# Even layer of a two-layer sequence trunk: zeros stored in a tap table, tap matrices read back shifted, and the attention bias spread before the stream

## The chip, the cores and the metric

The kernel runs on one core of one Trainium2 chip. The metric is the device time of one execution in microseconds (us). Engines are named as in the profile: PE (TensorE matmul), PEld (TensorE weight load), DVE (VectorE), ACT (ScalarE), POOL (GpSimd) and SP (SyncE, which here issues nearly all DMAs).

## The reference

Two residual layers over a sequence of 2048 tokens of width 1024, float32, and a final norm. The change is in layer 0, the even layer:

```python
h = rmsnorm(x, norm_w[0])
u, g_a, q, k, v, g_b = split_cols(h @ ev_w_in, [512, 512, 512, 128, 128, 512])
a_out = s5_mixer(u, ...) * silu(g_a)           # 32 groups of 16 channels, one 64-dim complex state each
b_out = swa_mixer(q, k, v, sinks, rel_bias) * silu(g_b)
x = x + concat([a_out, b_out]) @ ev_w_out
# s5_mixer: bu = B_bar u;  states = scan(lam_bar, bu);  y = Re(C states) + d * u;  gelu, half-GLU
# rel_bias[h, q, j] = table[bucket(j - 64 - q), h]   (64 queries against 128 keys)
```

Layer 1, the odd layer, is gated linear attention; the change does not touch it.

## The kernel before

**Loop of the even layer.** The input projection is cut into 72 products `n` (18 column groups of 128, times 4 blocks of 512 tokens). Each product is 24 matmuls 128x512 and is written as two half steps, `p = 2n` and `p = 2n + 1`. Every engine has its own hand-written loop over `p` from 12 to 147 (SP line 507, ACT 828, DVE 1110, PE 1284), and other work is hung on given values of `p`: so the order of work on an engine, and in SP's DMA queue, is fixed by these loops, and the engines meet at semaphores. PE does the half product first and then the small work of its `p`.

**Start.** 16 tiles of `x` (128 tokens each) are loaded into three buffers (`load_x`), squared on ACT (`square`, L680), scaled on DVE (`normed`, L885), turned by PE (`turn_x`, L1176), and split into a rounded part on ACT (`upper`, L686) and a rest on DVE (`lower`, L891). The products start when four tiles are through. SP's order at the start is `x` tiles 0 to 2 with two weight blocks, then zeros into the pads of `k_pad` and `v_pad` (L495) and one store of zeros over all 32 tap matrices (L496, 2048 KB), then `x` tile 3 (lines 486 to 499). ACT's second evacuation waits for these zeros, because they lie in its staging tile (L703).

**S5 tables, p = 16 to 50.** The S5 layer works on blocks of 8 steps. For each of 32 groups it needs a 128x384 table in DRAM (`scr["tab"]`): the input matrix (`bm`), the tap matrix (block Toeplitz: block column k is the row of 8 taps shifted by 16 k, zeros ahead of it) and the output matrix (`cp`). They are made for two groups at a time, 16 batches `q`, each batch two half steps: DVE makes powers (`powers_of_b` L989 to 991 at `p = 16 + 2q`, `powers_of_c` L1004 to 1006 at 17), PE turns (`turn_b` L1204, 17) and multiplies (`taps` L1212, 18), ACT copies (`copy_bm` L742, 17; `copy_ker` L748, 18), DVE adds the skip term (`skip` L1016, 19), SP stores (`store_cp` L379, 17; `store_bm` L374, 18; `store_toep`, 20). `store_toep` runs for odd `q` alone: 8 DMAs for the four groups of two batches, one for each shift:

```python
dst = scr["tab"][2 * q - 2:2 * q + 2].rearrange("g p c -> p g c")
for k in range(TS):
    sp.dma_start(dst[k * GRP:(k + 1) * GRP, :, P + k * GRP:2 * P], ker[:, :, 0:P - k * GRP]).then_inc(toep_st, 16)
```

The tap tile `ker` holds two batches. So `copy_ker` of an even `q` waits until the 8 stores of the two batches before it have landed (L747), and `taps(q)` on PE waits for `copy_ker(q - 1)`. POOL makes cosine and sine tables in the same stretch, until 161 us.

**Stream, p = 37 to 139.** For each group `i`, at three half steps each, SP loads the table row (L405), cosines and sines (L406, one 64-row table read twice) and inputs (L409); the request waits until PE has done the outputs of group `i - 2` (`y_done`). PE multiplies (`inputs` L1221 at `p = 40 + 3i`, `outputs` L1228 and L1229 three half steps later), ACT and DVE do scan and gelu (`take_v`, `scan`, `turn_back`, `gelu_out`), SP stores (`store_g`).

**Attention, p = 76 on.** Ahead of it, at `p = 53`, `set_attention` loads the bias table, a one-hot matrix and four pieces of the sinks; `distances` on PE (L1233, p = 55) and DVE (L1060, p = 56) forms the bias by distance (8 heads x 191), `spread_distances` (L431, p = 57) stores it 64 times over, 382 KB, and `load_bias` (L442, p = 61) reads it back shifted.

Of the kernel before, what the change touches and what calls it, by code (L numbers as in the profile page):

```python
# [17 lines left out]
P = 128  # L18
# [3 lines left out]
NT = SEQ // P  # L22
# [11 lines left out]
GPI = 4  # L34
GLU_C = BLK // TS
# [141 lines left out]
def even_layer(nc, prm, scr, ht_hi, ht_lo, cst, base, glu):  # L177
# [46 lines left out]
    with ExitStack() as ctx:  # L224
# [14 lines left out]
        zeros = stage[:, 3, 0:P]  # L239
# [54 lines left out]
        table, oneh, dvec = (at("at_table", B + 24, [BUCKETS, HEADS]), at("at_onehot", B + 24.75, [BUCKETS, NREL]),  # L294
                             at("at_by_distance", B + 25.5, [HEADS, NREL]))
# [12 lines left out]
        ps_d = bank[2][0:HEADS, 0:NREL]  # L308
# [9 lines left out]
         bx_ready, zero_in, bp_ready, b_turned, bm_ready, bst, cp_ready, k_done, ker_copied, ker_ready, cqst, toep_st,  # L318
# [3 lines left out]
            "k_done", "ker_copied", "ker_ready", "cqst", "toep_st", "cs_made"))  # L322
        cs_st = c.sems("s5_cs_st", 2)
# [5 lines left out]
        (set_in, dist_ready, dist_sb, dist_out, bias_in, achain, s_done, m_ready, e_done, r_ready, p_ready, p_turned,  # L329
         pt_ready, v_turned, v_ready, o_done, o_read) = (c.sem("at_" + n) for n in (  # L330
            "set_in", "dist_ready", "dist_sb", "dist_out", "bias_in", "chain", "s_done", "m_ready", "e_done",
# [7 lines left out]
        CS_ALL, TAB_ALL, TOEP_ALL = 16 * 8, 16 * NQ, 128 * (NQ // 2)  # L339

        with nc.Block() as block:
            @block.sync
            def _(sp):
# [32 lines left out]
                def store_cp(q):  # L376
                    dst = scr["tab"][2 * q:2 * q + 2].rearrange("g p c -> p g c")
                    sp.wait_ge(cp_ready, q + 1)
                    sp.dma_start(dst[:, :, 2 * P:3 * P], cp[:, :, 1:, :].rearrange("p g s i -> p g (s i)")).then_inc(cqst, 16)  # L379
# [14 lines left out]
                def load_stream(i):  # L394
# [9 lines left out]
                    sp.wait_ge(toep_st, 128 * (i // 4 + 1))  # L404
                    sp.dma_start(tab[:, j], scr["tab"][i]).then_inc(ld[j], 16)  # L405
# [9 lines left out]

                def set_attention():
                    sp.wait_ge(bst, TAB_ALL)
                    sp.wait_ge(cqst, TAB_ALL)
                    sp.wait_ge(toep_st, TOEP_ALL)
                    with nc.allow_non_contiguous_dma(reason="small parameters"):  # L420
                        sp.dma_start(table[:], prm["rel_bias_table"]).then_inc(set_in, 16)
# [1926 lines left out]
```

## Time and profile before

| | us |
|---|---|
| runs before, median of 3 (lowest to highest) | 1743.18 (1741.81 to 1743.65) |
| the profiled execution's own time | 1737.88 |
| its span, first to last instruction | 1736.1 |
| busy in the span: PE, DVE, ACT, POOL | 1651.5, 855.7, 630.5, 282.0 |
| mean granted TensorE clock | 0.990 |

PE is busy for 95% of the span. The even layer's loop lies between 38 and 612 us, the odd layer behind it. Each row of the trace gives start, duration, engine, line, operation and tile; a bracket at the end is the idle time of the engine ahead of it and what ended it.

### The profile page before, as it was taken

The page shows a single profiled execution, that of the slowest core. Times are in us where ns is not written, and L with a number is a line of the kernel's source. Part 1 is how long each engine was busy: PE and PEld are TensorE (multiplying, and loading weights), DVE is VectorE, ACT ScalarE, POOL GpSimd, SP SyncE. Part 2 cuts the span into 40 slices and gives each one's busy share as a digit, 9 for nine tenths or more (in the row PEclk, how much of TensorE's full clock was granted, in tenths as well). Part 3 has the DMA queues.
Part 4 walks back from the last instruction along what each step waited for, and adds up shares of the span by engine and source line. Part 5 has one row for each costly group of instructions (what it writes and reads, how often), then busy time and mean ns, then how long its engine had stood idle before and what let it go on. Part 6 is the DMA issues. An engine that isn't in the chain of part 4 may idle for free.

```text
span 1736.1 us, 22665 instructions
## 1 busy us (share of the span) xinstructions
PE 1651.5 (95%) x7910; PEld 1336.4 (77%) x7910; DVE 855.7 (49%) x1704; ACT 630.5 (36%) x1586; POOL 282.0 (16%) x500
## 2 busy tenths in 40 slices
PE   3998889999999979999999999999999999999997
PEld 2776667777777757888768888888888888878886
DVE  4868543476676556553363333333433444354443
ACT  4622233466666655332263122222222332132221
POOL 1866000000000071110000022221222211000000
PEclk9999989999999989999999999999999999999999
DMA  7335444454445595322233333333333332366663
GB/s 220 124 118 164 121 134 124 143 151 151 135 141 151 156 274 180 137 87 84 99 104 117 118 106 125 103 109 111 106 125 101 99 118 82 104 214 193 193 194 109
DMA packets 272009, 235.51 MB, mean 136 GB/s; under 512 B 81752, under 2 KB 225048, under 8 KB 271896
## 3 DMA queue, kind: packets, MB, share of 16 engines
q1 hardware_dynamic: 260600, 232.94, 42.8%
q10 hardware_dynamic: 11296, 1.12, 0.5%
q8 instruction: 64, 1.05, 0.3%
q14 instruction: 49, 0.40, 0.1%
HBM read 140.09 MB, written 93.91 MB: 135 GB/s over the span
## 4 chain that ended last, share of the span: by engine, by line
PE 61%; DVE 1%; ACT 1%; DMA 0%; issue 0%; POOLq 0%; POOL 0%; ACTq 0%; DVEq 0%
PE odd_bank L2140 29%; PE odd_bank L2186 10%; PE odd_bank L2295 10%; PE odd_bank L2165 2%; PE odd_bank L2245 2%; PE odd_bank L2242 1%; PE odd_bank L2243 1%; PE odd_bank L2224 1%; PE odd_bank L2149 1%; PE odd_bank L2200 1%; PE odd_bank L2226 0%; PE odd_bank L2253 0%; PE odd_bank L2227 0%; PE odd_bank L2252 0%; PE odd_bank L2228 0%; DMA scr_heads<-odd_ga_min 0%
## 5 line engine op out<-in xcount | busy, mean ns | idle before, releaser
L2140 PE MATMUL odd_bank<-ht_hi,odd_w_hi 128*128 128x512 f32 x768 | 318.4, 415 | 0.0
L2140 PE MATMUL odd_bank<-ht_lo,odd_w_hi 128*128 128x512 f32 x768 | 300.5, 391 | 0.0
L2140 PE MATMUL odd_bank<-ht_hi,odd_w_lo 128*128 128x512 f32 x768 | 298.9, 389 | 0.0
L1185 PE MATMUL ev_acc<-ht_hi,ev_w_hi 128*128 128x512 f32 x576 | 241.7, 420 | 1.8 <-DVE ht_lo L891 1.8
L1185 PE MATMUL ev_acc<-ht_hi,ev_w_lo 128*128 128x512 f32 x576 | 228.7, 397 | 0.0
L1185 PE MATMUL ev_acc<-ht_lo,ev_w_hi 128*128 128x512 f32 x576 | 228.3, 396 | 0.0
L1916 DVE COPY odd_stage<-odd_bank 128x512 f32<-128x512 f32 x96 | 66.4, 692 | 223.7 <-PE odd_bank L2140 223.7
L2140 PEld LDWEIGHTS odd_bank<-ht_lo,odd_w_hi 128*128 128x128 f32 x768 | 144.1, 188 | 31.8
L2140 PEld LDWEIGHTS odd_bank<-ht_hi,odd_w_hi 128*128 128x128 f32 x768 | 144.4, 188 | 29.9 <-issue 3.0
L2140 PEld LDWEIGHTS odd_bank<-ht_hi,odd_w_lo 128*128 128x128 f32 x768 | 144.6, 188 | 27.8
L1185 PEld LDWEIGHTS ev_acc<-ht_hi,ev_w_hi 128*128 128x128 f32 x576 | 110.2, 191 | 30.9 <-issue 4.3
L1185 PEld LDWEIGHTS ev_acc<-ht_lo,ev_w_hi 128*128 128x128 f32 x576 | 110.0, 191 | 25.2
L1185 PEld LDWEIGHTS ev_acc<-ht_hi,ev_w_lo 128*128 128x128 f32 x576 | 110.3, 191 | 20.0
L1838 ACT ACTIVATE odd_gl_o<-odd_bank 128x256 f32<-128x256 f32 x64 | 24.7, 386 | 241.9 <-DVE odd_gl_state L1972 228.6
L2295 PE MATMUL odd_bank<-ht_hi,odd_mf_hi 128*128 128x512 f32 x256 | 99.8, 390 | 1.2 <-DVE ht_lo L2109 1.2
L2295 PE MATMUL odd_bank<-ht_hi,odd_mf_lo 128*128 128x512 f32 x256 | 99.6, 389 | 0.0
L2295 PE MATMUL odd_bank<-ht_lo,odd_mf_hi 128*128 128x512 f32 x256 | 99.6, 389 | 0.0
L652 POOL TENSOR_TENSOR ht_lo_raw<-ht_lo_raw,glu_g_raw 128x512 f32<-128x512 f32 x4 | 9.2, 2333 | 447.9 <-DMA glu_g_raw<-scr_g 447.9
L1769 ACT ACTIVATE ht_hi<-odd_bank,odd_small 128x128 fp32r<-128x128 f32 x128 | 34.9, 382 | 128.4 <-PE odd_bank L2200 128.4
L2186 PE MATMUL odd_bank<-odd_wo_hi,ht_hi 128*128 128x512 f32 x256 | 80.1, 394 | 0.0
L2186 PE MATMUL odd_bank<-odd_wo_hi,ht_lo 128*128 128x512 f32 x256 | 79.0, 390 | 0.0
L2186 PE MATMUL odd_bank<-odd_wo_lo,ht_hi 128*128 128x512 f32 x256 | 78.9, 389 | 0.0
(285 smaller groups left out, 2921.4 us busy)
## 6 DMA issues: line engine op xcount, KB each, us to landing
odd_gl_in<-scr_heads SPq DMA_DIRECT2D x32, 640.0 KB, 4.2
scr_heads<-odd_stage SPq DMA_DIRECT2D x64, 256.0 KB, 2.0
odd_w_raw<-od_w_in SPq DMA_DIRECT2D x48, 256.0 KB, 3.5
ev_w_raw<-ev_w_in SPq DMA_DIRECT2D x36, 256.0 KB, 4.6
ev_x_tile<-x SPq DMA_DIRECT2D x16, 512.0 KB, 3.6
ev_s_cos_sin<-scr_s_cos_sin SPq DMA_DIRECT2D x32, 256.0 KB
odd_xo_sum<-x SPq DMA_DIRECT2D x16, 512.0 KB, 4.2
scr_x<-odd_xo_sum SPq DMA_DIRECT2D x16, 512.0 KB, 2.8
```

Of the source, the lines that this page charges most:

```text
L1185: mm = pe.matmul(acc[n % 3][:], w[j][:, k, :], h[:, k, t], start=(k == 0 and r == 0), stop=(k == KT - 1 and r == 2))
L1769: op = s.activation(ht_hi[:, 4 * h + k, t], pt[h][:, k], ACT.Copy, scale=norm_col[:, 4 * h + k:4 * h + k + 1])
L1838: s.activation(on[:, j], ps_o[j], ACT.Square, scale=DV ** -0.5, accum_out=ss[:, j:j + 1]).then_inc(ss_done, 1)
L1916: v.tensor_copy(stage[:, n % 4], acc[n % 4][:]).then_inc(acc_free, 1)
L2140: mm = pe.matmul(acc[n % 4][:], w[j][:, k, :], h[:, k, t], start=(k == 0 and q == 0), stop=(k == KT - 1 and q == 2))
L2149: mm = pe.matmul(acc[n][0:4 * RANK], w_low[:, k], h[:, k, cols(b)], start=(k == 0 and q == 0), stop=(k == KT - 1 and q == 1))
L2165: mm = pe.matmul(glu_acc[i % 3][:], w[:, 4 + k, at_:at_ + P], x, start=(k == 0 and r == 0), stop=(k == 3 and r == 2))
L2186: mm = pe.matmul(out_acc[2 * j + q][:], x[:, k, t], w[k][:, q * BLK:(q + 1) * BLK], start=(k == 0 and r == 0), stop=(k == KT - 1 and r == 2))
L2200: mm = pe.transpose(pt[h][:, k], hn[:, (4 * h + k) * P:(4 * h + k + 1) * P], ident[:])
L2224: pe.matmul(ps_att[:, q * CHUNK:(q + 1) * CHUNK], kk[:, s, p, q:q + 2].rearrange("p a t -> p (a t)"), qg[:, s, p * P + q * CHUNK:p * P + ( ...
L2245: pe.matmul(ps_s[j], kv[:, j, 0], values, start=True, stop=True).then_inc(st_done, 1)
L2295: mm = pe.matmul(facc[2 * j + q], mt[j][:, k], wt[:, k, part], start=(k == 0 and r == 0), stop=(k == KT - 1 and r == 2))
```

## The change

- **Zeros.** They get a tile of their own (46.25 KB into the arena) and are stored after the `x` loads, behind the evacuation of product 4 (`store_zeros`), into a new DRAM array `scr["toep"]` of 32 groups x 16 rows x 8 copies x 240 columns: 112 zeros in front of every copy, 4096 pieces of 448 bytes. ACT no longer waits for them; `load_stream` does.
- **Taps.** `store_toep` runs for every `q`, with two DMAs, one for each group: the 16 rows of taps, each written 8 times (64 KB). `copy_ker(q)` waits for the stores of batch `q - 2` alone.
- **Load.** A group's table is loaded by two DMAs in place of one: 128x256 (input and output matrix) and 128x128, the taps, each of the 8 blocks of rows read 16 columns earlier than the one before it. A stream step has four loads in place of three.
- **Bias by distance.** The bias table and the one-hot matrix are loaded at p = 13 (`load_distances`), multiplied on PE at p = 18, copied on DVE at p = 19 and spread at p = 21 in place of 53, 55, 56 and 57. `gelu_out` of the first two groups waits for the spread store, since it lies in that tile. `set_attention` keeps the four sink loads.

```diff
+AHEAD = P - GRP
+STRIDE = P + AHEAD
-        zeros = stage[:, 3, 0:P]
+        zeros = at("zeros", 46.25, [P, P])
...
                 def store_toep(q):
                     sp.wait_ge(ker_ready, q + 1)
-                    sp.wait_ge(zero_in, 16)
-                    dst = scr["tab"][2 * q - 2:2 * q + 2].rearrange("g p c -> p g c")
-                    for k in range(TS):
-                        sp.dma_start(dst[k * GRP:(k + 1) * GRP, :, P + k * GRP:2 * P],
-                                     ker[:, :, 0:P - k * GRP]).then_inc(toep_st, 16)
+                    for j in range(2):
+                        sp.dma_start(scr["toep"][2 * q + j][:, :, AHEAD:STRIDE],
+                                     ker[:, 2 * (q % 2) + j].unsqueeze(1).broadcast_to([GRP, TS, P])).then_inc(toep_st[q % 2], 16)
...
-                    sp.wait_ge(toep_st, 128 * (i // 4 + 1))
-                    sp.dma_start(tab[:, j], scr["tab"][i]).then_inc(ld[j], 16)
+                    q = i // 2
+                    sp.wait_ge(toep_st[q % 2], 32 * (q // 2 + 1))
+                    sp.wait_ge(zero_in, 16)
+                    sp.dma_start(tab[:, j, 0:2 * P], scr["tab"][i]).then_inc(ld[j], 16)
+                    shifted = scr["toep"][i].rearrange("i k c -> i (k c)")[:, AHEAD:AHEAD + TS * (STRIDE - GRP)]
+                    sp.dma_start(tab[:, j, 2 * P:3 * P], shifted.rearrange("i (k c) -> k i c", k=TS)[:, :, 0:P]).then_inc(ld[j], 16)
...
+                def store_zeros():
+                    sp.wait_ge(zero_made, 1)
+                    sp.dma_start(scr["toep"].rearrange("g i k c -> (g i k) c").rearrange("(p m) c -> p m c", p=P)[:, :, 0:AHEAD],
+                                 zeros[:, 0:AHEAD].unsqueeze(1).broadcast_to([P, NGRP, AHEAD])).then_inc(zero_in, 16)
+                    for pad in (scr["k_pad"], scr["v_pad"]):
+                        sp.dma_start(pad[:, 0:CHUNK], zeros[:, 0:CHUNK]).then_inc(pad_in, 16)
+                def load_distances():
+                    sp.wait_ge(ssq_done, NT)
+                    sp.dma_start(table[:], prm["rel_bias_table"]).then_inc(dist_in, 16)
+                    sp.dma_start(oneh[:], prm["onehot"]).then_inc(dist_in, 16)
...
                 load_w(1)
-                sp.wait_ge(zero_made, 1)
-                for pad in (scr["k_pad"], scr["v_pad"]):
-                    sp.dma_start(pad[:, 0:CHUNK], zeros[:, 0:CHUNK]).then_inc(pad_in, 16)
-                sp.dma_start(scr["tab"].rearrange("g p c -> p g c")[:, :, P:2 * P],
-                             zeros.unsqueeze(1).broadcast_to([P, NGRP, P])).then_inc(zero_in, 16)
                 for t in range(XB, 7):
                     load_x(t)
...
                         store_acc(n - 1)
+                store_zeros()
                 for p in range(12, p_end):
...
-                    if q is not None and q % 2 == 1:
+                    if q is not None:
                         store_toep(q)
...
-                    if p == TB + 2 * NQ + 9:
+                    if p == 13:
+                        load_distances()
+                    if p == TB + 5:
                         spread_distances()
...
-                    if q % 2 == 0 and q:
-                        act.wait_ge(toep_st, 128 * (q // 2))
+                    if q >= 2:
+                        act.wait_ge(toep_st[q % 2], 32 * (q // 2))
...
-                    if p == TB + 2 * NQ + 8:
+                    if p == TB + 3:
                         distances()
...
-                    pe.wait_ge(ld[j], 48 * (i // 2 + 1))
+                    pe.wait_ge(ld[j], 64 * (i // 2 + 1))
...
                 def distances():
-                    pe.wait_ge(set_in, 96)
+                    pe.wait_ge(dist_in, 32)
+                    pe.wait_ge(y_ready, 2)
...
-                    if p == TB + 2 * NQ + 7:
+                    if p == TB + 2:
                         distances()
```

## Rows read from the trace of the kernel before

**Rows 1.** Page, part 1: busy time, share of the span, instructions.
```profile
PE 1651.5 (95%) x7910; PEld 1336.4 (77%) x7910; DVE 855.7 (49%) x1704; ACT 630.5 (36%) x1586; POOL 282.0 (16%) x500
```

**Rows 2.** PE's waits for DVE's powers of C: total us, times, longest us.
```profile
PE ev_bank L1212 <- DVE ev_s_cpow L1006: 10.8, 6, 3.9
```

**Rows 3.** Start, x tiles: DMA issue to landing, of all 16 loads.
```profile
DMA to landing us min/median/max: 3.1/3.6/11.0
```

**Rows 4.** Timeline of ACT at the start: start us, us, operation, idle before and releaser.
```profile
27.78 1.06 ACT L680 ACTIVATE ev_x_squares<-ev_x_tile 128x1024 bf16<-128x1024 f32 x1 [6.62 <-DMA ev_x_tile<-x]
...
29.91 1.28 ACT L730 ACT_TABLE_LOAD   x1
...
32.89 1.06 ACT L680 ACTIVATE ev_x_squares<-ev_x_tile 128x1024 bf16<-128x1024 f32 x1
```

**Rows 5.** Timeline of PE at the start.
```profile
24.30 1.06 PE L1176 MATMUL ev_score_banks<-const_ident,ev_x_tile 128*128 128x128 f32 x4
```

**Rows 6.** DMA issues: the zero store, KB, us to landing.
```profile
scr_s_tables<-ev_stage SPq DMA_DIRECT2D x1, 2048.0 KB, 10.1
```

**Rows 7.** Timeline of PE: four idle stretches between 86 and 612 us.
```profile
190.91 1.01 PE L1212 MATMUL ev_bank<-ev_s_cpow,ev_s_bbar 128*16 128x128 f32 x4 [3.59 <-ACT ev_s_kernel L748]
227.65 1.04 PE L1212 MATMUL ev_bank<-ev_s_cpow,ev_s_bbar 128*16 128x128 f32 x4 [3.91 <-DVE ev_s_cpow L1006]
256.19 0.48 PE L1233 MATMUL ev_score_banks<-ev_at_onehot,ev_at_table 32*8 32x191 f32 x2 [1.87 <-DMA ev_at_small<-swa_sinks]
280.87 0.70 PE L1221 MATMUL ev_bank<-ev_s_u,ev_s_tables 128*128 128x256 f32 x2 [3.84 <-DMA ev_s_u<-scr_u]
```

**Rows 8.** Windows behind these: us, busy PE, PEld, DVE, ACT, POOL; PEclk, DMA share, GB/s.
```profile
190.90:197.00 6.10, 6.09 (x18) 4.48 (x19) 4.24 (x12) 2.65 (x7) 0.00 (x0) 0.56 0.74 186
227.60:235.00 7.40, 7.35 (x23) 5.59 (x23) 1.96 (x8) 1.48 (x4) 0.00 (x0) 0.58 0.61 166
256.20:262.00 5.80, 5.80 (x19) 4.36 (x20) 3.38 (x9) 1.24 (x3) 0.00 (x0) 0.71 0.58 177
280.80:286.00 5.20, 5.13 (x16) 4.08 (x17) 2.46 (x6) 2.23 (x6) 0.00 (x0) 0.67 0.32 98
```

**Rows 9.** Timeline of ACT: the tap copies ahead of the first two stretches.
```profile
190.40 0.36 ACT L748 COPY ev_s_kernel<-ev_bank 16x256 f32<-16x256 f32 x1 [11.66 <-DMA scr_s_tables<-ev_s_kernel]
...
222.65 0.36 ACT L748 COPY ev_s_kernel<-ev_bank 16x256 f32<-16x256 f32 x1 [5.88 <-DMA scr_s_tables<-ev_s_kernel]
```

**Rows 10.** Waits from 86 to 270 us, ACT's longest: total us, times, longest us.
```profile
ACT ev_s_kernel L748 <- DMA scr_s_tables<-ev_s_kernel: 54.5, 7, 12.1
```

**Rows 11.** Timeline of SP: the spread store and the table load behind it.
```profile
261.33 3.20 SPq L431 DMA_DIRECT2D scr_bias_by_distance<-ev_at_by_distance  x1
...
267.85 3.64 SPq L405 DMA_DIRECT2D ev_s_tables<-scr_s_tables  x1
```

**Rows 12.** Timeline of SP in the table stage.
```profile
121.51 3.62 SPq L386 DMA_DIRECT2D scr_s_tables<-ev_s_kernel  x8
```

**Rows 13.** Windows: the spread store in the DMA queue; the cosine load in it.
```profile
270.00:272.00 2.00, 2.00 (x11) 1.65 (x10) 1.47 (x4) 0.72 (x2) 0.00 (x0) 1.00 0.42 52
372.00:376.00 4.00, 4.00 (x25) 2.92 (x25) 2.91 (x7) 1.89 (x6) 0.00 (x0) 1.00 0.15 58
```

**Rows 14.** One line's instructions: SP's issue of an input load, ns min/median/max.
```profile
L409 SPq DMA_DIRECT2D ev_s_u<-scr_u x32: 589/596/1282, 180.4 to 563.7; - x32
```

**Rows 15.** Timeline of SP: requests of stream steps 4 and 12.
```profile
234.94 0.34 SPq L405 DMA_DIRECT2D ev_s_tables<-scr_s_tables  x1
...
321.49 0.39 SPq L405 DMA_DIRECT2D ev_s_tables<-scr_s_tables  x1
```

**Rows 16.** Timeline of PE: the inputs of these two steps.
```profile
244.25 0.59 PE L1221 MATMUL ev_bank<-ev_s_u,ev_s_tables 128*128 128x256 f32 x2
...
331.57 0.70 PE L1221 MATMUL ev_bank<-ev_s_u,ev_s_tables 128*128 128x256 f32 x2 [0.83 <-DMA ev_s_u<-scr_u]
```

**Rows 17.** One line's instructions, the bias loads of 32 KB: DMA issue to landing.
```profile
DMA to landing us min/median/max: 2.6/2.7/5.2
```

More of the change, by code:

```diff
@@ L293, in even_layer @@
         mx, mmx, sd, es, sm, rd = two(1), two(3), two(5), two(7), two(9), two(11)
-        table, oneh, dvec = (at("at_table", B + 24, [BUCKETS, HEADS]), at("at_onehot", B + 24.75, [BUCKETS, NREL]),
-                             at("at_by_distance", B + 25.5, [HEADS, NREL]))
+        table, oneh, dvec = (at("at_table", 46.75, [BUCKETS, HEADS]), at("at_onehot", A + 16.25, [BUCKETS, NREL]),
+                             at("at_by_distance", A + 17.25, [HEADS, NREL]))
         acc = [c.ps(f"acc{b}", [P, BLK]) for b in range(3)]
@@ L328, in even_layer @@
         g_st = c.sems("s5_g_st", 2)
-        (set_in, dist_ready, dist_sb, dist_out, bias_in, achain, s_done, m_ready, e_done, r_ready, p_ready, p_turned,
+        (set_in, dist_in, dist_ready, dist_sb, dist_out, bias_in, achain, s_done, m_ready, e_done, r_ready, p_ready, p_turned,
          pt_ready, v_turned, v_ready, o_done, o_read) = (c.sem("at_" + n) for n in (
-            "set_in", "dist_ready", "dist_sb", "dist_out", "bias_in", "chain", "s_done", "m_ready", "e_done",
+            "set_in", "dist_in", "dist_ready", "dist_sb", "dist_out", "bias_in", "chain", "s_done", "m_ready", "e_done",
             "r_ready", "p_ready", "p_turned", "pt_ready", "v_turned", "v_ready", "o_done", "o_read"))
@@ L418, in set_attention @@
                     sp.wait_ge(cqst, TAB_ALL)
-                    sp.wait_ge(toep_st, TOEP_ALL)
+                    for k in range(2):
+                        sp.wait_ge(toep_st[k], TOEP_ALL)
                     with nc.allow_non_contiguous_dma(reason="small parameters"):
-                        sp.dma_start(table[:], prm["rel_bias_table"]).then_inc(set_in, 16)
-                        sp.dma_start(oneh[:], prm["onehot"]).then_inc(set_in, 16)
                         sk = prm["swa_sinks"].rearrange("o (kv pair jp) -> o jp kv pair", kv=2, jp=2)
@@ L1090, in take @@
                     d.tensor_copy(o[:, u % 2, :, k * CHUNK:(k + 1) * CHUNK], ps_o).then_inc(o_read, 1)
-                d.memset(zeros, 0.0).then_inc(zero_made, 1)
+                d.memset(zeros[:], 0.0).then_inc(zero_made, 1)
                 rest = set_up()
@@ L1227, in outputs @@
                         pe.wait_ge(g_ready, i)
-                    pe.matmul(ps_y, tab[:, j, P:2 * P], ut[:, j], start=True, stop=False)
-                    pe.matmul(ps_y, tab[:, j, 2 * P:3 * P], pz[:, 0:NC], start=False, stop=True).then_inc(y_done, 1)
+                    pe.matmul(ps_y, tab[:, j, 2 * P:3 * P], ut[:, j], start=True, stop=False)
+                    pe.matmul(ps_y, tab[:, j, P:2 * P], pz[:, 0:NC], start=False, stop=True).then_inc(y_done, 1)
                 def distances():
-                    pe.wait_ge(set_in, 96)
+                    pe.wait_ge(dist_in, 32)
+                    pe.wait_ge(y_ready, 2)
                     pe.matmul(ps_d, table[:], oneh[:], start=True, stop=True).then_inc(dist_ready, 1)
```

21 lines of the change are left out of this document (10 added, 11 removed).

## The prediction

> **What bounds the kernel now.** I read the page's busy times first: PE is busy for 95% of the span [rows 1]. So a change of DMAs can pay only where PE stands idle or runs at the lower of its two clock levels, and the timeline of PE says where that is. Between the start of the products and 612 us four stretches matter: 3.59, 3.91, 1.87 and 3.84 us idle [rows 7]. After each the granted clock is at the half level for a while: the windows behind them show mean clocks of 0.56, 0.58, 0.71 and 0.67 while PE is busy with hardly a break [rows 8], a mix of 1.2 and 2.4 GHz. What a window loses to the clock is its length times what is missing to 1: 6.10 x 0.44 = 2.7, 7.40 x 0.42 = 3.1, 5.80 x 0.29 = 1.7 and 5.20 x 0.33 = 1.7 us.
>
> What ends these stretches comes from ACT's and SP's views. The first ends with ACT's copy of a tap tile, which had waited 11.66 us for tap stores to land. The second is named after DVE, but DVE's work there hung on ACT's `take_v`, queued behind another such copy that waited 5.88 us [rows 9]. In all ACT stands 54.5 us in 7 such waits [rows 10]. The third ends with the sink loads, issued behind the bias table in one bundle. The fourth ends with a stream load: its table was requested at 267.85, and the issue alone took 3.64 us, in place of the 0.34 of another step, because the spread store of 261.33 held the queue [rows 11, 15]. At 270 to 272 us the DMA engines are busy for 0.42 and move 52 GB/s [rows 13]; at that rate the 382 KB of that store take 7.3 us.
>
> PE's other waits of the table stage are for DVE's powers: 10.8 us [rows 2], of which 3.91 are the second stretch. The other 7 us are DVE's own pace while POOL works too, and the change doesn't touch them.
>
> **The change part by part.**
>
> *Zeros behind x.* The median x load lands after 3.6 us, the longest after 11.0 [rows 3]. That one is tile 3, behind 2048 KB of zeros that take 10.1 us [rows 6]; ACT waits 6.62 us for it, until 27.78 [rows 4]. At 3.6 us it would be there 7.4 us sooner, by 20.4. Then the next thing is late: ACT's `upper(2)`, two copies, needs PE's second turn, which ends at 24.30 + 1.06 = 25.4 [rows 5]. The copies take 29.91 - 27.78 - 1.06 = 1.07 us together, and the second ends at about 26. From the table load at 29.91 to the next square at 32.89 are 2.98 us [rows 4]: so that square comes at 29.0 to 29.1, and everything behind it on ACT, DVE and PE is a chain. The products start **3.8 us earlier**; bounds 2 (another load late) and 6.6 (the whole wait). In SP's queue the moved store passes thirteen x loads, a weight block and two stores of u. Behind it then stand two u stores, the small distance loads and the next weight block. The first of them that anybody needs is a u store, by ACT's evacuation of product 8, some 7 half steps later: 22 us, at a third of step 4's 9.31 us each [rows 15, 16]. The store's 10.1 us are covered, even twice over: 0. Without that cover it would cost what it overran.
>
> *Tap stores.* 8 DMAs for two batches become 2 for each batch, and a copy waits for stores issued two half steps (6 us) before it. The eight took 3.62 us of SP [rows 12]; four cost half. Stretches 1 and 2 go: 3.59 + 2.7 + 3.91 + 3.1 = **13.3 us**. Next in line are the stores of `cp` and `bm`, each out of a single buffer; behind a stream load they land late, and PE's 6 us between two `taps` have to cover that.
>
> *Distances early.* Stretch 3 goes, 1.87 + 1.7 = **3.6 us**: PE waits for nothing loaded at `p = 53` any more. Its 0.48 us matmul [rows 7] and DVE's copy are the same work elsewhere, and the new wait of `gelu_out` was met long before. Stretch 4 goes, 3.84 + 1.7 = **5.5 us**, because the spread store no longer stands ahead of a stream load. It stands at `p = 21`, behind a wait for DVE's copy, ahead of `store_toep(1)`, `store_bm(2)`, `store_cs(2)` and `store_cp(3)`. SP's own time there is even: 3.20 us for it at most, less the 2.7 that six tap stores fewer save. But it holds the queue for 7.3 us, and ACT's `copy_bm(3)`, POOL's fifth table and DVE's `powers_of_c(4)` wait for stores behind it. DVE is the slow engine there, so part of this reaches PE: between 0 and 6 us. I take **+1.0**, near the lower end, because while POOL waits, DVE is faster.
>
> *One more load in a stream step.* The request stands behind PE's outputs two groups before. In step 4 PE comes for the data 9.31 us after the request (234.94 to 244.25) without a wait; in step 12 it comes 10.08 us after (321.49 to 331.57), 0.83 of which is a wait for the landing [rows 15, 16]. So the load chain takes 9 to 10 us where PE's work takes 9.3: nearly balanced over steps 4 to 12, until attention makes PE's steps longer. The cosine load is the longest part of the chain: at 372 to 376 us, while it runs, the DMA engines are busy for only 0.15 [rows 13], some 2 of 16; cosines and inputs are issued behind the new load. That adds its issue, 0.34 as for a table load [rows 15] or 0.60 as for an input load [rows 14], and at most a whole landing of 2.7, which the 32 KB bias loads take alone [rows 17]. I take 0.6, the issue of the load whose pattern it shares (8 blocks of 16 rows). Half of it is slack in the mean: 9 steps x 0.3, about **+2.5 us**. The Trainium skill, "DMA: Bandwidth & Descriptors", section Rules for kernel authors, wants many small transfers coalesced, since under 64 KB one pays mostly overhead; here 64 KB are split off a larger load. Were that overhead wholly in line, the sum would be that of the slower rival below.
>
> *The first stream load* hid behind stretch 1. Its input load is issued at 180.4 [rows 14], the table some 1.1 us before; with 9.3 to 10.1 us and 0.6 it lands at 189.2 to 190.0. PE comes to it at 190.91 - 3.59 + 0.6 = 187.9. Bounds 0 and 2.1; **+1.0**.
>
> Sum: -3.8 - 13.3 - 3.6 - 5.5 + 1.0 + 2.5 + 1.0 = **-21.7 us**. The profiled execution took 1737.88 (span 1736.1), 5.3 below the median of the runs, and comes to 1716.2 on its own time; on the median to 1743.18 - 21.7 = **1721.5**.
>
> **Rivals.**
> - *The table stage gives back.* The spread store at `p = 21` opens a new idle stretch with a half clock behind it, like the one that it removes: +5.5 in place of +1.0, and the start gains 2 in place of 3.8: -15.4, 1728. For it: DVE is the slow engine there. Against: POOL is held as well.
> - *Another store takes the taps' place.* If `bm` and `cp` stores behind stream loads hold ACT or DVE, stretches 1 and 2 only halve: -15.0, 1728. For it: they share the queue with the slow cosine load. Against: they do so now, and none of the four stretches ends on them.
> - *The start gains nothing*, because what holds x is not the zeros: 1725. Against: only one load takes 11.0.
> - *Slower: the stream's load chain becomes the bound.* If the new load adds 2.7 us, the nine balanced steps lose 9 x 2.4 = 22, and each idle of that size may draw a half clock of 1.7 us behind it, as stretch 3 did: 15 more. The 19 attention steps last (562.6 - 321.49) / 19 = 12.7 us [rows 14, 15], so 10.1 + 2.7 costs them some 0.3 each, 6. That is +43 in place of +2.5: -21.7 + 40.5 = +19, 1762. It decides from 1.3 us a step if each idle draws a half clock, from 2.7 if none does. Against: loads overlap in the queue.
>
> **How the numbers follow.** A measurement of this kernel tells about 0.2%, 3.5 us, from no change. Forecast 0.65; table stage 0.13; other stores 0.11; start 0.05; slower 0.04; within 0.2% by a mixture 0.02. Faster 0.94, same 0.02, slower 0.04. The range takes in the cases at 1728 with 3 us for the first load and the stream, and below the forecast the new costs at nothing (-4.5) and a start that gains more (up to 2.8): 1713 to 1731.
>
> **What would show it.** Right: PE's products start near 34 us; ACT waits under 2 us for tap stores; no idle row of PE over 1.5 us between 165 and 612 us, and clock 1.00 there; the stream loads are PE's commonest releaser, under 1 us each. Wrong: a new stretch near 120 us; a half clock in the stream; PE's waits for `ev_s_u` over 10 us in sum.

## The result and the profile after

The changed kernel takes **1732.24 us** (median of 4 runs, 1731.70 to 1732.70) against 1743.41 us before (4 runs): a ratio of 0.9937, interval 0.9923 to 0.9951. That is 11.2 us faster, half of the 21.7 forecast, and 1.2 us above the upper end of the range. The profiled execution took 1732.69 us, span 1730.9, so here the profile stands for the median; that of before stood 5.5 us under its own. In the two profiles the first matmul behind the even layer's loop starts at 623.08 us before and at 614.91 after: 8.2 us earlier. What lies behind it, which no edit touches, took 1113.0 and 1116.0 us.

The page, part 1, of the changed kernel (busy us, share of the span, instructions):

```profile
PE 1651.8 (95%) x7910; PEld 1335.9 (77%) x7910; DVE 858.8 (50%) x1704; ACT 630.7 (36%) x1586; POOL 279.8 (16%) x500
```

PE does the same work as before [rows 1]; what changed is its idle time and its clock. The timeline of PE shows where (start us, us, operation, idle time before it and what ended it):

```profile
33.01 1.12 PE L1188 MATMUL ev_bank<-const_ident,ev_x_tile 128*128 128x128 f32 x4 [4.12 <-DVE ev_x_tile L895]
...
151.40 1.03 PE L1224 MATMUL ev_bank<-ev_s_cpow,ev_s_bbar 128*16 128x128 f32 x4 [2.97 <-DVE ev_s_cpow L1016]
...
188.73 0.70 PE L1233 MATMUL ev_bank<-ev_s_u,ev_s_tables 128*128 128x256 f32 x2 [1.45 <-DMA ev_s_u<-scr_u]
...
201.86 1.22 PE L1233 MATMUL ev_bank<-ev_s_u,ev_s_tables 128*128 128x256 f32 x2 [2.08 <-DMA ev_s_u<-scr_u]
...
238.61 0.70 PE L1233 MATMUL ev_bank<-ev_s_u,ev_s_tables 128*128 128x256 f32 x2 [2.83 <-DMA ev_s_u<-scr_u]
...
271.77 0.70 PE L1233 MATMUL ev_bank<-ev_s_u,ev_s_tables 128*128 128x256 f32 x2 [1.94 <-DMA ev_s_u<-scr_u]
```

None of the four stretches of before [rows 7] is left: no copy of taps, no sinks, no spread store ends an idle time of PE any more, and ACT's list of waits from 86 us on has no tap store in it, where it had 54.5 us [rows 10]. Part of that moved to the stores of `bm`: from 178 to 280 us ACT waits for them for 14.4 us in 3 places, where it was 2.9 us in one before.

```profile
ACT ev_s_bmat L752 <- DMA scr_s_tables<-ev_s_bmat: 14.4, 3, 5.6
```

But no idle time of PE over 0.5 us ends there. In the stream PE now waits mainly for the stream loads. PE's longest waits from 165 to 420 us and in the table stage from 100 to 165 us (total us, times, longest us):

```profile
PE ev_bank L1233 <- DMA ev_s_u<-scr_u: 11.0, 8, 2.8
```

```profile
PE ev_bank L1224 <- DVE ev_s_cpow L1016: 5.3, 3, 3.0
PE ev_score_banks L1216 <- DVE ev_s_bpow L1001: 3.2, 2, 1.7
```

And three windows of 5 to 7 us behind the rows of 151.40, 201.86 and 238.61 (columns as in [rows 8]):

```profile
150.00:157.00 7.00, 5.60 (x15) 4.11 (x16) 6.90 (x8) 0.36 (x1) 6.77 (x6) 0.54 0.34 87
201.00:206.00 5.00, 4.14 (x11) 3.35 (x12) 2.31 (x7) 1.40 (x4) 0.00 (x0) 0.66 0.29 71
238.00:243.00 5.00, 4.39 (x12) 3.54 (x13) 2.32 (x6) 1.54 (x4) 0.00 (x0) 0.66 0.28 95
```

There the granted clock is 0.54, 0.66 and 0.66, a mix of the two levels, so 7 x 0.46 = 3.2 us (a little less, as PE still stands idle in the first 1.4 of the 7) and twice 5 x 0.34 = 1.7 us are lost.

Why the waits for loads are long is to be seen in SP's timeline ahead of stream steps 1 and 4, whose requests are the rows of L407 at 192.31 and 228.87:

```profile
185.23 3.84 SPq L358 DMA_DIRECT2D ev_w_raw<-ev_w_in  x2
189.11 2.40 SPq L386 DMA_DIRECT2D scr_s_taps<-ev_s_kernel  x2
...
192.31 0.36 SPq L407 DMA_DIRECT2D ev_s_tables<-scr_s_tables  x1
...
221.48 3.56 SPq L358 DMA_DIRECT2D ev_w_raw<-ev_w_in  x2
225.09 2.98 SPq L386 DMA_DIRECT2D scr_s_taps<-ev_s_kernel  x2
...
228.87 0.35 SPq L407 DMA_DIRECT2D ev_s_tables<-scr_s_tables  x1
```

The same weight loads in the kernel before, SP's timeline:

```profile
191.75 1.19 SPq L356 DMA_DIRECT2D ev_w_raw<-ev_w_in  x2
...
228.55 1.65 SPq L356 DMA_DIRECT2D ev_w_raw<-ev_w_in  x2
...
256.72 4.56 SPq L356 DMA_DIRECT2D ev_w_raw<-ev_w_in  x2
```

Two weight DMAs take SP 3.84 and 3.56 us to issue where they took 1.19 and 1.65 before. They come 4.2 and 3.0 us behind the issue of the last load of the step before; in the old kernel PE had stood idle just then, and it was 10.7 and 4.8 us. The third row, 256.72, stands 1.2 us behind such loads, and there the old kernel took 4.56 us too. So both requests come late. From request to landing step 1 takes 201.86 - 192.31 = 9.55 us and step 4 238.61 - 228.87 = 9.74, no more than the 10.08 of step 12 before [rows 15, 16]; but PE comes for the data 7.47 and 6.91 us after the request, where in step 4 before it came after 9.31 [rows 15, 16], and waits 2.08 and 2.83 us. That the cosine load is what makes the weight loads slow is the theory of the first experiment.

### The profile page after: what moved, and what is told of

The parts are those of the page before. It is cut to its first block, busy times and chain, and to the rows that moved or that the text cites. A ratio compares the mean times of both kernels' runs of the same rounds, so it can differ in the third digit from the quotient of the medians.

```text
span 1730.9 us, 22673 instructions
## 1 busy us (share of the span) xinstructions
PE 1651.8 (95%) x7910; PEld 1335.9 (77%) x7910; DVE 858.8 (50%) x1704; ACT 630.7 (36%) x1586; POOL 279.8 (16%) x500
## 4 chain that ended last, share of the span: by engine, by line
PE 61%; DVE 1%; ACT 1%; issue 1%; DMA 0%; POOLq 0%; POOL 0%; ACTq 0%; DVEq 0%
PE odd_bank L2153 29%; PE odd_bank L2199 10%; PE odd_bank L2308 10%; PE odd_bank L2178 2%; PE odd_bank L2258 2%; PE odd_bank L2255 2%; PE odd_bank L2256 1%; PE odd_bank L2237 1%; PE odd_bank L2162 1%; PE odd_bank L2213 1%; PE odd_bank L2239 0%; PE odd_bank L2266 0%; PE odd_bank L2265 0%; PE odd_bank L2240 0%; PE odd_bank L2241 0%
```

## The experiments

Fifteen variants ran beside the kernel before; each ratio is against that kernel's runs of the same session (their medians lay between 1741.5 and 1744.7).

```
run                  edit                                   median us   ratio [95% interval]
(changed kernel)                                             1732.24    0.9937 [0.9923, 0.9951]
e1_cs_two            cosine load in two DMAs                 1720.10    0.9869 [0.9853, 0.9885]
e2_shift_last        shifted taps last, awaited later        1734.07    0.9945 [0.9930, 0.9960]
e3_behind            weights, taps behind the stream load    1732.78    0.9939 [0.9923, 0.9955]
e4_zeros             before + zeros moved                    1738.91    0.9974 [0.9965, 0.9984]
e5_before_cs_two     before + cosine load in two DMAs        1730.05    0.9919 [0.9903, 0.9934]
e6_dist_late         distances back at their old place       1735.71    0.9959 [0.9945, 0.9973]
e7_more_loads        one more load in a stream step          1738.32    0.9973 [0.9963, 0.9983]
e8_cs_two_bias       e1 + bias loads later                   1712.76    0.9823 [0.9810, 0.9837]
e9_queue             e3 + two weight loads moved             1734.46    0.9956 [0.9942, 0.9970]
e10_spread_early     distances 5 half steps earlier          1731.93    0.9944 [0.9930, 0.9959]
e11_cs_bias_spread   e8 + e10                                1717.30    0.9852 [0.9836, 0.9869]
e12_cs_bias_late     e8 + e6                                 1717.44    0.9856 [0.9838, 0.9873]
e13_cs_bias_first    e8 + distances ahead of the stage       1710.53    0.9820 [0.9803, 0.9836]
e14_first            distances ahead of the stage            1729.40    0.9927 [0.9913, 0.9941]
e15_no_shifted       added load left out from step 2 on      1727.93    0.9909 [0.9890, 0.9928]
```

**Is it the load chain? (e1_cs_two)**

```diff
-sp.dma_start(cs[:, j]..., scr["cs"][i]....unsqueeze(0).broadcast_to([2, ST, 2 * NC])).then_inc(ld[j], 16)
+for h in range(2):
+    sp.dma_start(cs[h * ST:(h + 1) * ST, j], scr["cs"][i]).then_inc(ld[j], 16)
...
-pe.wait_ge(ld[j], 64 * (i // 2 + 1))
+pe.wait_ge(ld[j], 80 * (i // 2 + 1))
```

> Changed kernel, but the cosines and sines of a stream step come by two DMAs of 64 partitions each in place of one DMA that repeats 64 rows. Theory (the chain of a stream step's loads became PE's bound once the tap stores were out of the way, and the cosine load, which kept only some 2 of 16 DMA engines busy, is its longest part): PE's waits for the stream loads, 11.0 us in 8 places in the changed kernel, fall under 2 us, the two half clocks of 3.4 us each in the stream go, and the time falls by 11 + 3.4 = 14 us, from 1732 to about 1718. Rival (the table stage took the gain back: its idle time and the half clock of 6.8 us at 150 us, worth 3.4): the stream is not what holds it, and the time stays within 2 us, 1730 to 1732.

1720.10 us, 12.1 less than the changed kernel. SP's timeline, at the two places shown above:

```profile
185.37 1.17 SPq L358 DMA_DIRECT2D ev_w_raw<-ev_w_in  x2
...
188.91 0.36 SPq L407 DMA_DIRECT2D ev_s_tables<-scr_s_tables  x1
...
214.98 1.18 SPq L358 DMA_DIRECT2D ev_w_raw<-ev_w_in  x2
...
219.51 0.35 SPq L407 DMA_DIRECT2D ev_s_tables<-scr_s_tables  x1
```

The weight loads are issued in 1.17 and 1.18 us, the requests come in time, and PE waits for no stream load at all from 165 to 420 us. What is left there is one wait of PE, and it is for something else (waits of PE in this stretch; its longest row):

```profile
PE ev_bank L1239 <- DVE ev_s_out L1067: 4.8, 4, 4.0
```

```profile
279.34 1.02 PE L1239 MATMUL ev_bank<-ev_s_u,ev_s_tables 128*128 128x256 f32 x2 [3.96 <-DVE ev_s_out L1067]
```

So the theory holds: the cosine load is the longest part of the chain, and it also holds SP's queue for what is issued behind it. The old load repeats 64 rows; while it runs alone the DMA engines are busy for 0.15 [rows 13], 0.15 x 16 = 2.4, so some two of 16. Of stream step 16, 5.6 to 7.6 us after the request, the share was 0.13 before, and in e1_cs_two it is 0.03 from 5.8 to 7.8 us: there the loads are through. The Trainium skill, "DMA: Bandwidth & Descriptors", section Rules for kernel authors, says that a leading broadcast of c copies confines a DMA to at most c engines; here c is 2, and the share of 0.13 to 0.15 agrees.

**Was it slow before, too? (e5_before_cs_two)** The same edit in the kernel before.

> Kernel before, with the cosine load in two DMAs of 64 partitions, as in e1_cs_two. Theory (in the kernel before the stream loads' length was hidden under the stretches that other things made): PE waited only 5.0 us for stream loads there, 3.84 of them behind the spread store; the gain is 1.2 to 5.0 us plus at most one half clock of 1.7, 1736.5 to 1742, and so the change is worth 16 to 22 us on top of it. Rival (the faster load is worth the same with and without the change, and its 12 us have nothing to do with the forecast's miss): 1743 - 12 = 1731. Between them: the faster load also frees the queue for the tap stores, and the first two stretches shrink, by up to 7.5 us idle and 5.8 of clock.

1730.05 us, the rival's figure: the faster load alone is worth 13.4 us. PE's timeline says why:

```profile
223.47 1.03 PE L1211 MATMUL ev_bank<-ev_s_cpow,ev_s_bbar 128*16 128x128 f32 x4 [4.15 <-DVE ev_s_cpow L1005]
250.09 0.49 PE L1232 MATMUL ev_score_banks<-ev_at_onehot,ev_at_table 32*8 32x191 f32 x2 [0.64 <-DMA ev_at_small<-swa_sinks]
...
270.01 0.70 PE L1220 MATMUL ev_bank<-ev_s_u,ev_s_tables 128*128 128x256 f32 x2 [0.69 <-DMA ev_s_u<-scr_u]
```

The first stretch is gone, the third has 0.64 us left of 1.87 and the fourth 0.69 of 3.84; only the second stands, 4.15. So three of the four stretches hung on the queue that the cosine load held, the fourth too, although the spread store stands where it stood. The change took out what was queued (tap stores, sinks, spread), not what held the queue. My theory falls in the form that I had given it: it had the change worth 16 to 22 us on top of the fast load, and it is worth 1730.05 - 1720.10 = 10 (9 by the ratios).

**What is the added load worth? (e15, e7, e2)** Three edits of the load of the shifted taps: left out from step 2 on (the later steps use what lies in the buffers), split in two, and issued last with a semaphore of its own. The counts that PE waits for change with them and are not shown.

```diff
 e15_no_shifted
+if i < 2:
     sp.dma_start(tab[:, j, 2 * P:3 * P], ...).then_inc(ld[j], 16)
 e7_more_loads
-sp.dma_start(tab[:, j, 2 * P:3 * P], ...[:, :, 0:P]).then_inc(ld[j], 16)
+for h in range(2):
+    sp.dma_start(tab[h * ST:(h + 1) * ST, j, 2 * P:3 * P], ...[h * TS // 2:(h + 1) * TS // 2, :, 0:P]).then_inc(ld[j], 16)
 e2_shift_last
 sp.dma_start(ut[:, j], ...).then_inc(ld[j], 16)
+sp.dma_start(tab[:, j, 2 * P:3 * P], ...).then_inc(ld_k[j], 16)
...
 pe.wait_ge(pz_ready, i + 1)
+pe.wait_ge(ld_k[j], 16 * (i // 2 + 1))
```

> Changed kernel without the added load: the shifted taps are loaded in stream steps 0 and 1 alone, and steps 2 to 31 use what lies in the two buffers (their own shifted taps are left out). Prediction's term for the added load: 2.5 us, 1729.7. If one more load is worth what the doubling showed (e7_more_loads, 6.1 us): 1726. If the added load makes all the stream's new waits of steps 2 to 12 (7.5 us idle, 1.7 to 3.4 of clock): 1721 to 1723. If the waits come from the cosine load, which was slow in the kernel before too and was covered there by the four stretches, and the added load is free: 1731 to 1732, with steps 4 and 7 still late by 2 to 3 us.

> Changed kernel, with the load of the shifted taps split into two DMAs of 64 partitions: one more load in a stream step, as the change itself added one. If a load costs its issue, 0.6 us, in the steps where PE waits for loads (8 of them): 8 x 0.6 = 4.8 us more, 1737. If it costs half that, as the prediction took it (0.3 a step): 1734.7. If an added load is free, as the run with the shifted load at the end suggests: 1731 to 1733. If its whole landing of 2.7 counts: 1732 + 8 x 2.7 = 1754.

> Changed kernel, but the load of the shifted taps is issued last of the four and has a semaphore of its own, for which only the output products wait, three half steps later. If the issue of the new load, 0.6 us ahead of cosines and inputs, is what lengthened the chain: 8 waits get shorter by 0.6 us, 4.8 in sum, and at most one half clock goes with them, 1.7: 1726 to 1728. If the new load's whole landing stood in the line (2.7 us): all 8 waits go, with both half clocks, 1718 to 1720. If the chain was as long before, and only late requests in SP's queue made the long waits: under 2 us, 1730 to 1732.

Without the load the kernel takes 1727.93 us, 4.3 less; by the ratios it is 0.0028 of 1743, 4.9, but the two intervals overlap, so the size is rough. PE's waits from 165 to 420 us, and the three long ones:

```profile
PE ev_bank L1234 <- DMA ev_s_u<-scr_u: 8.3, 6, 2.4
```

```profile
199.21 1.19 PE L1234 MATMUL ev_bank<-ev_s_u,ev_s_tables 128*128 128x256 f32 x2 [2.38 <-DMA ev_s_u<-scr_u]
...
234.40 0.70 PE L1234 MATMUL ev_bank<-ev_s_u,ev_s_tables 128*128 128x256 f32 x2 [2.02 <-DMA ev_s_u<-scr_u]
...
265.47 0.70 PE L1234 MATMUL ev_bank<-ev_s_u,ev_s_tables 128*128 128x256 f32 x2 [1.45 <-DMA ev_s_u<-scr_u]
```

8.3 of the 11.0 us are still there. Of these, 1.31 and 2.38 are in steps 0 and 1, which still have the added load. Steps 4 and 7, whose chain is the old one, wait 2.02 and 1.45 us, and with two short waits in steps 6 and 12 that makes 4.6 us, where the changed kernel has 7.5 from step 2 on. Split in two, the load costs 6.1 us more, and the same row has 14.8 us in 10 waits:

```profile
PE ev_bank L1235 <- DMA ev_s_u<-scr_u: 14.8, 10, 3.5
```

So one load of this kind costs some 4 to 6 us over the stream; the split's interval is clear of the changed kernel's. Issued last it costs no less (1734.07, the intervals overlap): the short waits of steps 6 and 10 are gone, the long ones stand (2.20, 2.85 and 2.02 us in steps 1, 4 and 7), the wait of step 12 has grown from 0.87 to 1.63, and one of 1.51 us for DVE's `s_out` to 2.29. Where in the bundle it stands changes nothing that these runs can tell; that it is in the queue does.

**Does the order in SP's queue decide? (e3_behind, e9_queue)**

```diff
 e3_behind
-if p in LOAD_W: load_w(LOAD_W[p])
-if batch_at(p, TB + 4) is not None: store_toep(...)
...
 if i is not None: load_stream(i)
+if p in LOAD_W: load_w(LOAD_W[p])
+if batch_at(p, TB + 4) is not None: store_toep(...)
 e9_queue (as e3_behind, and)
-LOAD_W = {8 * (g - 1) - 2 * (g in (9, 17)): g for g in range(3, N_GRP)}
+LOAD_W = {8 * (g - 1) - 2 * (g in (7, 9, 17)) - (g == 8): g for g in range(3, N_GRP)}
```

> Changed kernel, but in a half step that has several of them SP issues the weight load and the tap stores behind the stream load and not ahead of it. If SP's queue made the long waits (the stream steps whose request stood behind a weight load and two tap stores waited 2.08, 2.83 and 1.94 us, and both half clocks stand behind the first two): these three waits fall under 0.8 us and the half clocks go: 6.85 - 2.4 + 3.4 = 8 us, 1724. If the length of the four loads themselves is the cause: the waits stay and the time is within 2 us, 1730 to 1732.

> Changed kernel; SP issues weight loads and tap stores behind the stream load of their half step, and the two weight loads that stood one and two half steps ahead of a late request (stream steps 4 and 7) go right behind the requests of steps 3 and 6. Only the order in SP's queue differs. Theory (the long waits, 2.08, 2.83 and 1.94 us in steps 1, 4 and 7, come from requests that stand behind weight loads whose issue takes 3.6 to 4.1 us): the three fall under 0.8 us in sum 4.5 us less, one or both half clocks of 3.4 go, 1.7 each: 1724 to 1728. Rival (the four loads are too long wherever the request stands; the weight loads only fill the queue at another place): 1731 to 1734.

1732.78 and 1734.46 us: neither gains. In e3_behind step 1 waits only 0.88 us in place of 2.08, but step 4 still waits 3.29 (its weight load stands one half step ahead of it, which this edit doesn't reach) and DVE's powers come late by 0.7 to 1.1 us three times. In e9_queue the weight load stands right behind the request of step 3. SP's timeline (this execution had a granted clock of 0.95 almost throughout, so only its order and its waits are read):

```profile
218.65 4.10 SPq L358 DMA_DIRECT2D ev_w_raw<-ev_w_in  x2
222.80 3.84 SPq L386 DMA_DIRECT2D scr_s_taps<-ev_s_kernel  x2
...
230.28 0.46 SPq L407 DMA_DIRECT2D ev_s_tables<-scr_s_tables  x1
```

The two weight DMAs now take 4.10 us and the taps behind them 3.84, ACT waits 7.20 us for tap stores, and step 4 waits 3.81. My theory of the order falls: the hold goes wherever the next DMA stands. What is late is the queue's content behind a slow load, not one request.

**What do the distances cost and give? (e6, e10, e14)** They go back to their old place, five half steps ahead, and ahead of the whole table stage.

```diff
 e6_dist_late: load_distances with the sinks (p == 53), matmul 55, copy 56, spread 57
 e10_spread_early
-if p == 13: load_distances()      # matmul 18, copy 19, spread 21
+if p == 12: load_distances()      # matmul 14, copy 15, spread 16
 e14_first (onehot and dvec in other free columns)
+if n == 4: load_distances()       # half step 8; matmul 11, copy ahead of 12, spread 12
```

> Changed kernel, with the table, the matmul, the copy and the spread of the bias by distance back at the half steps of the kernel before (loads with the sinks, spread behind them). Prediction's terms for this part: 3.6 + 5.5 - 1.0 = 8.1 us lost again, 1740. Rival (the spread at its early place costs the table stage an idle time and the half clock at 150 us, 3.4 us): 3.4 to 4 of the 8.1 come back, 1736.5, and the half clock at 150 us is gone. Rival of the masking kind (where the fourth stretch stands, PE no longer waits for stream loads of the next steps, 1.94 and 0.73): 1738.

> Changed kernel, with the bias by distance five half steps earlier: loads at half step 12, matmul at 14, copy at 15, spread store at 16, ahead of the first table stores and not among them. Theory (the spread at half step 21 costs the table stage far more than the 1.0 us forecast: from the first products to stream step 0 the changed kernel takes 154.3 us without its wait there, the run with the distances late 148.9): the stage gets 3 to 5 us shorter, 1727 to 1729. Rival (the table stage is longer for another reason, the two tap stores of every batch; the run with the distances late is only shifted): 1731 to 1733. Rival (it holds the queue at its new place for the first batches and a weight load just the same): 1732 to 1735.

> Changed kernel with the bias by distance ahead of the table stage, as in e13_cs_bias_first, and nothing else. Theory: 3 to 4.4 us shorter than the changed kernel, 1728 to 1729, the stream's waits of 11 us as before. Rival (an earlier stream step 0 only waits longer for its loads, which take their time from the tables stored last): 1731 to 1732.

Put back, they cost 3.5 us (1735.71) and not 8.1. PE's timeline of that run:

```profile
32.54 1.11 PE L1184 MATMUL ev_bank<-const_ident,ev_x_tile 128*128 128x128 f32 x4 [4.12 <-DVE ev_x_tile L893]
...
182.86 0.70 PE L1229 MATMUL ev_bank<-ev_s_u,ev_s_tables 128*128 128x256 f32 x2 [1.38 <-DMA ev_s_u<-scr_u]
...
273.58 1.22 PE L1229 MATMUL ev_bank<-ev_s_u,ev_s_tables 128*128 128x256 f32 x2 [9.18 <-DMA ev_s_u<-scr_u]
```

The fourth stretch is back, and longer, 9.18 us; but the table stage is shorter. From the first row to step 0, less PE's wait there, it takes 182.86 - 1.38 - 32.54 = 148.9 us; in the changed kernel 188.73 - 1.45 - 33.01 = 154.3. The half clock at 151 us, some 3 us, is within the 154.3. What the early spread does there is to be seen in the changed kernel's timelines of SP, ACT, POOL and DVE:

```profile
113.85 0.78 SPq L446 DMA_DIRECT2D scr_bias_by_distance<-ev_at_by_distance  x1
114.74 4.50 SPq L386 DMA_DIRECT2D scr_s_taps<-ev_s_kernel  x2
...
125.69 0.37 ACT L752 COPY ev_s_bmat<-ev_score_banks 128x256 f32<-128x256 f32 x1 [5.76 <-DMA scr_s_tables<-ev_s_bmat]
...
127.01 1.07 POOL L645 TENSOR_TENSOR ev_s_cs_made<-ev_s_coarse_r,ev_s_fine_r 128x512 f32<-128x512 f32 x1 [5.07 <-DMA scr_s_cos_sin<-ev_s_cs_made]
...
127.36 1.04 DVE L1014 TENSOR_TENSOR ev_s_cpow<-ev_s_pow_r,ev_s_cT 128x288 f32<-128x288 f32 x1 [4.34 <-DMA scr_s_tables<-ev_s_cpow]
```

The spread is issued in 0.78 us, but the two tap stores behind it take 4.50 (1.25 elsewhere), and ACT, POOL and DVE wait 5.76, 5.07 and 4.34 us for the `bm`, `cs` and `cp` stores: the three waits that the prediction named. Five half steps earlier the price is the same (1731.93), with other batches paying it. The timeline of e10_spread_early, DVE and POOL:

```profile
107.09 0.46 DVE L1014 TENSOR_TENSOR ev_s_cpow<-ev_s_pow_r,ev_s_cT 128x288 f32<-128x288 f32 x1 [7.93 <-DMA scr_s_tables<-ev_s_cpow]
...
108.81 1.19 POOL L645 TENSOR_TENSOR ev_s_cs_made<-ev_s_coarse_r,ev_s_fine_r 128x512 f32<-128x512 f32 x1 [14.26 <-DMA scr_s_cos_sin<-ev_s_cs_made]
```

Ahead of the stage it is gone: in e14_first step 0 comes 184.55 - 1.37 - 32.78 = 150.4 us after the same row, 3.9 less than in the changed kernel (timeline of PE):

```profile
32.78 1.12 PE L1187 MATMUL ev_bank<-const_ident,ev_x_tile 128*128 128x128 f32 x4 [4.12 <-DVE ev_x_tile L895]
...
184.55 0.70 PE L1232 MATMUL ev_bank<-ev_s_u,ev_s_tables 128*128 128x256 f32 x2 [1.37 <-DMA ev_s_u<-scr_u]
```

Both differences, 3.9 here and 154.3 - 148.9 = 5.4 us, still hold the half clock of the changed kernel's profile. e15_no_shifted has the spread at half step 21 and a granted clock of 1.00 at that place (149.8 to 157 us); its timeline of PE:

```profile
31.87 1.12 PE L1189 MATMUL ev_bank<-const_ident,ev_x_tile 128*128 128x128 f32 x4 [4.12 <-DVE ev_x_tile L896]
...
185.78 0.70 PE L1234 MATMUL ev_bank<-ev_s_u,ev_s_tables 128*128 128x256 f32 x2 [1.31 <-DMA ev_s_u<-scr_u]
```

That is 185.78 - 1.31 - 31.87 = 152.6 us, and e8_cs_two_bias below, also at 1.00 there, takes 185.37 - 32.09 = 153.3. Against the 148.9 of e6_dist_late, which has no half clock either, the spread costs 3.7 to 4.4 us. Of the time e14_first shows 2.8 us (1729.40), and its interval overlaps with the changed kernel's.

**The start alone (e4_zeros)**

```diff
+zeros = at("zeros", 46.25, [P, P])
-(stores of pads and zeros, ahead of x tile 3)
...
+(the same stores, behind the last load of x)
...
-(ACT's wait for them ahead of its second evacuation)
```

> Kernel before, with one part of the change alone: the zeros have a tile of their own and are stored behind the loads of x (still into the old tables). Theory (the start gains what the prediction said and what the changed trace shows, products 3.3 us earlier): 1743.4 - 3.5 = 1740, with products from about 34.7 us. Rival (an earlier start only lets PE wait longer in the table stage, whose powers don't come sooner): within 1 us of the kernel before, 1742.5 to 1743.5.

1738.91 us, 4.0 less, 4.5 by the ratio. PE's first product starts at 33.58 us in this profile (38.01 before, 34.71 in the changed kernel). The theory holds.

**A version that beats both (e8, e11, e12, e13)** The kernel of e1 with the bias loads behind the next stream request, and then with the distances at three other places.

```diff
-if p == TB + 2 * NQ + 13: load_bias()
+if p == TB + 2 * NQ + 17: load_bias()
```

> The kernel of e1_cs_two, with the eight bias loads issued four half steps later, behind the request of the stream step that follows. In e1_cs_two they hold SP's queue for 5 us ahead of a weight load, ACT waits 8.39 us for those weights, and PE 3.96 us behind ACT. Theory (that is the last large wait of the stream): 3.96 us and the clock behind it, 1.7 to 3.4, go: 1713 to 1715. Rival (the next request of a stream step or the next weight load is late in its place): 1719 to 1721.

> The kernel of e8_cs_two_bias with the bias by distance ahead of the table stage: loads at half step 8, matmul at 11, copy before half step 12, spread store at 12, behind the zeros. Theory (what it costs at 21 and at 16 is the hold of the first or third batch's stores; ahead of the stage nobody waits for what stands behind it): the table stage gets 3 to 4.4 us shorter: 1708 to 1710. Rival (zeros and spread together hold the queue into the first batches): 1713 to 1717. Rival (matmul and copy make PE or DVE wait at the end of the start): 1712 to 1714.

> The kernel of e8_cs_two_bias with the bias by distance back at its place of the kernel before, as in e6_dist_late: the spread store stands in the stream, where the queue is now free of the slow cosine load. Theory (the spread at half step 21 costs the table stage 4.4 us by holding the stores of cp and bm, and its old place was bad only beside the slow cosine load): the table stage gets 4.4 us shorter, the stream pays some 1.3 us for the sinks and a request (0.64 and 0.69 in e5_before_cs_two): 1709 to 1710. Rival (the spread holds the queue as long in the stream, and PE waits there for a stream load): 1713 to 1716.

> The kernel of e8_cs_two_bias with the bias by distance five half steps earlier, as in e10_spread_early. Theory: the table stage gets 3 to 5 us shorter and nothing hides it, since PE waits for no load in the stream: 1708 to 1710. Rivals as for e10_spread_early: 1712 to 1713, or 1713 to 1715.

e8_cs_two_bias takes 1712.76 us. Three windows of its stream (columns as in [rows 8]):

```profile
190.00:210.00 20.00, 20.00 (x93) 15.33 (x93) 13.14 (x37) 7.96 (x19) 0.00 (x0) 1.00 0.56 155
210.00:230.00 20.00, 20.00 (x91) 16.18 (x90) 9.02 (x26) 7.98 (x18) 0.00 (x0) 1.00 0.63 170
...
270.00:300.00 30.00, 30.00 (x134) 25.00 (x133) 13.63 (x33) 10.97 (x26) 0.00 (x0) 1.00 0.55 162
```

PE is busy for the whole of them at the full clock, as the prediction had wanted it of the changed kernel. With the distances ahead of the stage it is 1710.53; the ratios, 0.9820 and 0.9823, don't tell the two apart. The other two places are worse: the spread among the first batches 1717.30 (PE waits 2.77 and 1.14 us for DVE at 109.78 and 119.02), and in the stream 1717.44, with this row in PE's timeline:

```profile
256.21 0.70 PE L1228 MATMUL ev_bank<-ev_s_u,ev_s_tables 128*128 128x256 f32 x2 [2.85 <-DMA ev_s_u<-scr_u]
```

The spread holds a stream request there as it did before. In the profiles that only eats up what the shorter table stage gave: the first matmul behind the even layer's loop starts at 596.91 us against 596.55 in e8. Why the medians are 4.7 us apart is not settled; the profiles differ behind that matmul (1118.5 and 1113.5 us), where no edit touches the kernel.

## Why the prediction was wrong

The direction was right, and so was what each part takes away; the size was not. The steps that failed are two prices and one omission, and the omission is the largest.

- **Start, -3.8:** right. e4 measures -4.0 to -4.5, and PE's products start 4.4 us earlier there and 3.3 earlier in the changed kernel.
- **Stretches 1 and 2, -13.3, and 3 and 4, -9.1:** all four went, with their clock. ACT's waits for `bm` stores grew, as the prediction had feared, but no idle time of PE over 0.5 us in the stream ends on them. The length of 1, 2 and 4 was not the gain; see the last step.
- **Spread at half step 21, +1.0:** mis-sized, 3.7 to 4.4 us. The waits were named rightly and the bounds 0 to 6 held; "near the lower end, because while POOL waits, DVE is faster" was the wrong choice. ACT and DVE wait themselves (5.76 and 4.34 us).
- **One more load, +2.5, and the first load, +1.0:** the first load is right, 1.45 at step 0; the added load is mis-sized by some 2 us, since e15 gives 4.3 to 4.9 for the steps from 2 on. "Half of it is slack in the mean" was the weak point: in the steps that wait, the chain takes 9.5 to 10.5 us, and PE comes for the data 9.3 to 9.5 us after the request where that isn't held, sooner where it is. The Trainium skill, "DMA: Bandwidth & Descriptors", Rules for kernel authors, has transfers under 64 KB as mostly overhead; wholly in line, that overhead would have made the 43 us of the slower rival. The runs show 4 to 6.
- **Left out: what the stretches covered.** The sum took the whole length of stretches 1, 2 and 4 as gained, and asked of each only whether the next store would be late. But behind them the same slow queue stood. While PE waited for taps, the loads of the step before went on landing, and the weight load behind them was issued quickly (1.19 and 1.65 us); with the stretches gone, it is issued in 3.84 and 3.56 us, and steps 1, 4 and 7 wait for loads whose request is late. In e15 8.3 us of waits for stream loads are left: 1.31 in step 0, which is the term for the first load, 2.38 in step 1, which still has the added load, so that its own share isn't shown, and 4.6 behind it without that load. Before there were 0.35 in step 9 and 0.83 in step 12 [rows 16]; and one half clock, 1.7, comes with step 1: 8.3 - 1.2 + 1.7 = 8.8 us. The fourth stretch was such a wait from the start: its releaser in [rows 7] is a stream load, the weight load ahead of the spread took 4.56 us, and I took the spread for its whole cause. With a faster cosine load and the spread at its old place 0.69 of its 3.84 us are left (e5).

With these, the first load within the 8.8, the sum is -4.5 - 22.4 + 4 + 4.5 + 8.8 = -9.6 us, against -11.2 measured and -8.2 in the rows of the two profiles: as near as these runs can tell (the half clock at 150 us is left out on both sides, since executions of either kind of kernel show it or not). It is put together after the fact, and the terms are not independent: e1 and e5 show that the stretches and the new waits both hang on the same cosine load. Of the signs that the prediction had named for its failure, two are there: over 10 us of waits for `ev_s_u`, and a half clock in the stream. The third, a new stretch near 120 us, is not: from 100 to 165 us PE waits 9.4 us in all and waited 9.1 before. I had the rival "load chain becomes the bound" at 0.04 because I made it depend on the added load being slow; it needed no slower load, only requests that are held while PE no longer is. (Its 0.3 us for each attention step doesn't follow either: 10.1 + 2.7 against 12.7 is 0.1.)

The range failed for the same reason as the chances: two of the rivals' mechanisms, the table stage and the load chain, came at once, each at part of its size. I had priced each alone, with the rest of the sum intact.

## What to carry to other kernels

When a stall goes, its length is not the gain: ask what else was in flight during it, and what of that would end after the moment at which the stall now doesn't begin. A queue that is shared shows a slow transfer in the issue time of whatever stands behind it (here weight loads, 1.2 against 2.7 to 4.6 us). Here two reorderings of that queue only moved the hold, while loading the slow transfer by two DMAs without the repeat removed it. A term whose waits can be named, but not timed, belongs near the middle of its bounds.

## What the runs showed that I had not expected

- One edit of a load (two DMAs of 64 partitions for one that repeats 64 rows) is worth 12 to 13 us in either kernel, more than the change itself.
- Issuing the two weight DMAs took SP 1.17 us behind fast loads and 2.70 to 4.56 a few us behind a cosine load on some two engines.
- The clock behind the same idle time differs between executions: 2.97 us ahead of the `taps` matmuls at 151 us are followed by the lower level in the changed kernel (0.54 over 150 to 157 us) and in e1_cs_two, and not in e15_no_shifted (1.00 over 149.8 to 157 us) or in the kernel before, where the next rows run at full speed. A term for the clock behind one idle time of this size is a chance, not a price.
